# 31 panels of block 2 in high and low parts, the delta rule's inversion rounds in another order, and three norms run together

## The reference, cut to what matters

```
proj = h @ w_in                     # also the 3 x 1024 gate columns br_gate
y_a = mamba2_branch(...)
y_b = stick_breaking_branch(...)    # q, k = rms_norm(q), rms_norm(k), then attention
y_c = gated_deltanet_branch(...)    # o = rms_norm(delta rule) * silu(gate)
branch_proj = einsum("bsie,ied->bsid", stack([y_a, y_b, y_c]), w_branch)
merged = sum(sigmoid(br_gate) * branch_proj, axis=2)
x = x + gate_m * (merged @ w_out)
h = rms_norm(x) * (1 + scale_f) + shift_f
x = x + gate_f * hier_moe(h, ...)
```

## Time and profile before

| what | value |
|---|---|
| median of 3 runs | 1633.55 us (1627.95 to 1636.26) |
| profiled execution | 1627.25 us, its span 1625.4 us |
| TensorE busy | 1531.1 us (94% of the span) |
| VectorE, ScalarE, GpSimd busy | 714.0, 537.9, 217.3 us |
| mean granted TensorE clock | 0.968 of full speed |
| DMA | 375.76 MB, mean 231 GB/s |

### The profile page before, as it was taken

The page is one execution under the profiler, slowest core; times in us unless marked ns, Lnnn a source line. Parts: engine busy times, 40 slices in busy tenths (PEclk is TensorE's granted clock), DMA queues, the critical chain, the costliest instruction groups (busy, mean ns, idle before and its releaser), DMA issues.

```text
span 1625.4 us, 27552 instructions
## 1 busy us (share of the span) xinstructions
PE 1531.1 (94%) x11006; PEld 1262.3 (78%) x11006; DVE 714.0 (44%) x1309; ACT 537.9 (33%) x860; POOL 217.3 (13%) x90
## 2 busy tenths in 40 slices
PE   7988999999999999999989887998899999999997
PEld 5857999999768999989978876887666666566554
DVE  5954888558576888334535412312311111111111
ACT  2345545453445555366551105202111111111110
POOL 0011211212101212238650000000000000000000
PEclk9979999999999999989999968999799999999999
DMA  7674555664434565625441102344999999999995
GB/s 300 234 272 155 166 166 170 198 229 156 153 125 136 172 191 185 191 82 177 137 136 52 52 26 65 105 155 143 423 426 428 428 429 427 427 427 428 426 427 220
DMA packets 63740, 375.76 MB, mean 231 GB/s; under 512 B 7200, under 2 KB 7456, under 8 KB 48032
## 3 DMA queue, kind: packets, MB, share of 16 engines
q1 hardware_dynamic: 63648, 374.43, 61.3%
HBM read 373.35 MB, written 1.05 MB: 230 GB/s over the span
## 4 chain that ended last, share of the span: by engine, by line
PE 71%; issue 13%; DVE 7%; DMA 5%; ACT 3%; SPq 2%; POOL 0%; POOLq 0%; DVEq 0%; ACTq 0%
PE lin L648 7%; PE lin L649 7%; PE lin L650 7%; PE lin L667 6%; PE mixp L1241 6%; PE mixp L1245 6%; PE stat L1265 6%; DVE mixers L1844 3%; PE lin L1219 3%; PE lin L996 2%; DMA moe_arena<-in_experts 2%; DMA modrow<-in_experts 2%; PE stat L1210 2%; PE stat L648 1%; PE mixp L648 1%
## 5 line engine op out<-in xcount | busy, mean ns | idle before, releaser
L648 PE MATMUL lin<-r_hi,w_hi 128*128 128x256 f32 x1344 | 392.1, 292 | 9.4 <-POOL w_lo L1648 5.1
L649 PE MATMUL lin<-r_lo,w_hi 128*128 128x256 f32 x1344 | 382.6, 285 | 0.0
L650 PE MATMUL lin<-r_hi,w_lo 128*128 128x256 f32 x1344 | 382.4, 285 | 0.0
L648 PEld LDWEIGHTS lin<-r_hi,w_hi 128*128 128x128 f32 x1344 | 260.3, 194 | 17.3 <-POOL w_lo L1648 6.7
L649 PEld LDWEIGHTS lin<-r_lo,w_hi 128*128 128x128 f32 x1344 | 260.4, 194 | 0.8
L650 PEld LDWEIGHTS lin<-r_hi,w_lo 128*128 128x128 f32 x1344 | 260.2, 194 | 0.0
L1681 DVE TENSOR_TENSOR w_lo<-ring,w_hi 128x1024 fp32r<-128x1024 f32 x126 | 156.4, 1246 | 84.8 <-ACT w_hi L1312 65.2
L1648 POOL TENSOR_TENSOR w_lo<-ring,w_hi 128x1024 fp32r<-128x1024 f32 x42 | 108.3, 2579 | 480.2 <-ACT w_hi L1312 297.9
L2328 DVE TENSOR_TENSOR moe_arena<-moe_arena,mixp 128x256 f32<-128x256 f32 x32 | 13.5, 421 | 339.2 <-ACT moe_arena L1623 339.2
L1312 ACT ACTIVATE w_hi<-ring 128x1024 fp32r<-128x1024 f32 x124 | 129.6, 1048 | 57.4 <-PE mixp L650 50.0
L667 PE MATMUL lin<-h,ring 128*128 128x256 f32 x640 | 145.5, 385 | 3.0 <-DVE h L1712 3.0
(11 more groups left out here) (422 smaller groups left out, 2641.7 us busy)
## 6 DMA issues: line engine op xcount, KB each, us to landing
ring<-in_panels SPq DMA_DIRECT2D x272, 512.0 KB, 3.5
moe_arena<-in_experts SPq DMA_DIRECT2D x66, 2048.0 KB, 24.5
aring<-in_ada SPq DMA_DIRECT2D x24, 1024.0 KB, 6.1
ring<-in_experts SPq DMA_DIRECT2D x10, 2048.0 KB, 23.2
cst<-in_experts SPq DMA_DIRECT2D x10, 1280.0 KB, 23.0
sq<-in_experts SPq DMA_DIRECT2D x10, 1024.0 KB, 24.6
rs<-in_experts SPq DMA_DIRECT2D x10, 512.0 KB, 25.8
modrow<-in_experts SPq DMA_DIRECT2D x10, 512.0 KB, 28.0
```

Of the source, the lines that this page charges most:

```text
L648: pe.matmul(o, w_hi[:, slot, c], r[0], start=start, stop=False, skip_group_check=True)
L649: pe.matmul(o, w_hi[:, slot, c], r[1], start=False, stop=False, skip_group_check=True)
L650: return pe.matmul(o, w_lo[:, slot, c], r[0], start=False, stop=stop, skip_group_check=True)
```

## The change

`is_split` now also covers the last 31 panels of block 2: branch 2 from j = 1 on (11), branch 1 (12) and the output panels (8). GpSimd makes their low parts. ScalarE cuts a panel when the panel three places ahead of it has been read (`split_hi` in `gates`). Their right-hand sides are split as well: `h` into `r_hi` and `r_lo` behind the state loop, y_c and y_b into `y2_*` and `y1_*`, and `merged` into `c_hi` and `c_lo`, two tiles at a time (`round_merged`). They lie in SBUF where nothing is kept any more by then.

In an inversion round the filling panel moves to behind the first product, the product for `g_d` goes ahead of that for `g_dt`, and the mask of `g_ml` waits only for the first product.

The three norms run together: the Squares of q and k are taken ahead of the rounds, the sums of q, k and the output follow the state loop at once, then three Ln, three Exp and the Silu come in a row. The scaling of the delta rule's output moves behind that of q and k. `gate_branch(2, 0)` and `gate_branch(2, 1)` move behind the two steps of stick-breaking that followed them, and the filling panels are dealt out anew.

```diff
+BRANCHES2 = BRANCH2 + 13
...
-    return OUT0 <= n < BRANCH2
+    return OUT0 <= n < BRANCH2 or BRANCHES2 <= n < PANELS
...
+        with ExitStack() as under_sq:
+            y2_hi, y2_lo = (under_sq.enter_context(nc.sbuf_tensor(n, [P, KH, T], F32R)) for n in ("y2_hi", "y2_lo"))
...
+            with ExitStack() as branch_rows:
+                sb1("below_rows", [P, (8 + KH) * T], stack=branch_rows)
+                c_hi, c_lo = (sb1(n, [P, KD, T], F32R, branch_rows) for n in ("c_hi", "c_lo"))
+                y1_hi, y1_lo = (sb1(n, [P, KH, T], F32R, branch_rows) for n in ("y1_hi", "y1_lo"))
...
+        rs_k, rs_o = gq[:, 0:4, :], gq[:, 4:8, :]
...
-            def split_linear(b, first=False):
+            def split_linear(b, first=False, rows=(r_hi, r_lo)):
...
-                    mm = split_matmul(lin[b][:, 0:T], (b, slice(i * P, (i + 1) * P)), (r_hi[:, i, :], r_lo[:, i, :]),
+                    mm = split_matmul(lin[b][:, 0:T], (b, slice(i * P, (i + 1) * P)), [t[:, i, :] for t in rows],
...
-            def project(rhs):
+            def project(rows, first=False):
...
-                    linear(rhs, 1)
+                    b = split_panel()
+                    bank(b)
+                    split_linear(b, first and m == 0, rows)
+                    panels.advance(1)
...
-            project(None)
+            project((r_hi, r_lo))
...
-            project(None)
+            project((r_hi, r_lo))
...
-                    b = panel()
+                    split = is_split(panels.n)
+                    b = split_panel() if split else panel()
...
+                    if split and (i, j) in ((2, 1), (2, 3), (1, 0)):
+                        pe.wait_ge(h_ready, seen(h_ready, KD if j == 1 else 1))
...
-                        product(b, h)
+                        if split:
+                            split_linear(b)
+                        else:
+                            product(b, h)
+                    elif split:
+                        for m in range(2):
+                            for k in range(KH):
+                                at = (2 * k + m) * P
+                                mm = split_matmul(lin[b][:, m * T:(m + 1) * T], (b, slice(at, at + P)),
+                                                  [t[:, k, :] for t in ((y2_hi, y2_lo) if i == 2 else (y1_hi, y1_lo))],
+                                                  k == 0, k == KH - 1)
+                        mm.then_inc(panel_done, 1)
...
+                branch_panels(0, 3 + n, 4 + n)
...
-                for i, s in blocks:
-                    mm = pe.matmul(stat[:, i, s], g_w[:, i, s], g_dt[:, i, s], start=True, stop=True, skip_group_check=True)
-                mm.then_inc(ev("g_ddt_ready"), 1)
+                if n > 1:
+                    pe.wait_ge(ev("g_dt_ready"), n - 1)
...
-                branch_panels(0, 3 + n, 4 + n)
+                for i, s in blocks:
+                    mm = pe.matmul(stat[:, i, s], g_w[:, i, s], g_dt[:, i, s], start=True, stop=True, skip_group_check=True)
+                mm.then_inc(ev("g_ddt_ready"), 1)
...
+            def head_sums(src, dst):
+                pe.wait_ge(sq_ready, seen(sq_ready))
+                for i in range(4):
+                    mm = pe.matmul(dst[:, i, :], K["ones"], src[:, i, :], start=True, stop=True, skip_group_check=True)
+                mm.then_inc(sums_ready, 1)
+            logs = seen.now(ln_done)
+            head_sums(sq[:, 0:4, :], mixp)
+            pe.wait_ge(ev("g_o_read"), 1)
+            head_sums(sq[:, 4:8, :], stat)
+            pe.wait_ge(ln_done, logs + 1)
+            head_sums(sq[:, 0:4, :], mixp)
+            seen(ln_done, 3)
...
-            pe.wait_ge(ev("g_o_read"), 1)
-            sums(sq, 4, 1)
-            branch_panels(0, 11, 12)
-            sums(sq, 4, 1)
-            pe.wait_ge(ev("yc_done"), 1)
-            branch_panels(2, 0, 2)
-            sums(sq, 4, 1)
+            pe.wait_ge(ln_done, logs + 3)
...
-            branch_panels(2, 2, 3)
+            branch_panels(0, 11, 12)
...
-            branch_panels(2, 3, 6)
+            pe.wait_ge(ev("yc_done"), 1)
+            branch_panels(2, 0, 5)
...
-            branch_panels(2, 6, 8)
+            branch_panels(2, 5, 8)
...
-            project(merged)
+            project((c_hi, c_lo), True)
...
+                    if i != BRANCHES[0]:
+                        split_hi(panels.n + RING - 1)
+            def round_merged(pair, behind):
+                panels.taken(-behind)
+                tiles = slice(2 * pair, 2 * pair + 2)
+                act.activation(c_hi[:, tiles, :], merged[:, tiles, :], ACT.Copy).then_inc(r_hi_ready, 1)
...
+            for half in range(2):
+                tiles = slice(4 * half, 4 * half + 4)
+                act.activation(sq[:, tiles, :], sq_kv[:, tiles, :], ACT.Square).then_inc(sq_ready, 1)
...
-            gates(0, 9, 11)
+            gates(0, 9, 10)
+            act.wait_ge(ev("g_o_ready"), 4)
+            for half in range(2):
+                tiles = slice(4 * half, 4 * half + 4)
+                act.activation(r_hi[:, tiles, :], h[:, tiles, :], ACT.Copy).then_inc(r_hi_ready, 1)
+            def log_sums(dst, src):
+                act.wait_ge(sums_ready, seen(sums_ready))
+                act.activation(dst, src, ACT.Ln, bias=K["eps"], scale=1.0 / P).then_inc(ln_done, 1)
+                seen(ln_done)
+            log_sums(rs[:, :, :], mixp[:, :, :])
...
-            norm(ybr[:, 8:12, :], 4, 4, P)
-            gates(0, 11, 12)
+            act.activation(sq[:, 0:4, :], ybr[:, 8:12, :], ACT.Square).then_inc(sq_ready, 1)
+            log_sums(rs_k, stat[:, :, :])
+            log_sums(rs_o, mixp[:, :, :])
+            act.wait_ge(ln_done, seen.now(ln_done))
+            for t in (rs[:, :, :], rs_k, rs_o):
+                act.activation(t, t, ACT.Exp, scale=-0.5).then_inc(rs_ready, 1)
...
+            next_split[0] = BRANCHES2
+            split_hi(BRANCHES2 + 2)
+            gates(0, 10, 12)
...
-            norm(sq_kv[:, 0:4, :], 4, 4, P)
-            gates(2, 0, 2)
-            act.wait_ge(ev("b_normed"), 1)
-            norm(sq_kv[:, 4:8, :], 4, 4, P)
-            gates(2, 2, 3)
+            act.activation(y2_hi[:, :, :], ybr[:, 8:12, :], ACT.Copy).then_inc(r_hi_ready, 1)
+            split_hi(BRANCHES2 + 3)
...
-            gates(2, 3, 6)
+            split_hi(BRANCHES2 + 4)
+            gates(2, 0, 5)
...
-            gates(2, 6, 12)
-            gates(1, 0, 12)
+            gates(2, 5, 9)
+            act.wait_ge(ev("yb2_done"), 1)
+            act.activation(y1_hi[:, :, :], ybr[:, 4:8, :], ACT.Copy).then_inc(r_hi_ready, 1)
+            gates(2, 9, 12)
+            gates(1, 0, 6)
+            round_merged(0, 6)
+            gates(1, 6, 9)
+            round_merged(1, 6)
+            gates(1, 9, 12)
+            round_merged(2, 6)
+            round_merged(3, 3)
...
-            for n in range(CHAIN2, BRANCH2):
+            for n in (*range(CHAIN2, BRANCH2), *range(BRANCHES2, PANELS)):
...
-                dve.wait_ge(ev("g_ddt_ready"), n)
...
+                    dve.wait_ge(ev("g_w_ready"), n)
...
-                    link(dve.tensor_tensor(g_dt, g_dt, stat[:, :, :], ALU.subtract))
...
+                    dve.wait_ge(ev("g_ddt_ready"), n)
+                    dve.tensor_tensor(g_dt, g_dt, stat[:, :, :], ALU.subtract).then_inc(ev("g_dt_ready"), 1)
...
+                    dve.wait_ge(ev("g_dt_ready"), n)
...
+                    dve.wait_ge(ev("g_ddt_ready"), n)
...
-            dve.wait_ge(ev("g_o_read"), 1)
-            dve.wait_ge(rs_ready, seen(rs_ready))
-            link(dve.scalar_tensor_tensor(ybr[:, 8:12, :], ybr[:, 8:12, :], col("gdn_norm"), rs[:, :, :], ALU.mult, ALU.mult))
-            dve.wait_ge(ev("gg_ready"), 1)
-            dve.tensor_tensor(ybr[:, 8:12, :], ybr[:, 8:12, :], gg, ALU.mult).then_inc(ev("yc_done"), 1)
-            gate_branch(0, 3)
+            for half in range(2):
+                tiles = slice(4 * half, 4 * half + 4)
+                dve.wait_ge(r_hi_ready, seen(r_hi_ready))
+                dve.tensor_tensor(r_lo[:, tiles, :], h[:, tiles, :], r_hi[:, tiles, :].bitcast(F32), ALU.subtract)\
+                    .then_inc(h_ready, 4)
...
-            dve.scalar_tensor_tensor(sq_kv[:, 4:8, :], sq_kv[:, 4:8, :], col("sb_kn"), rs[:, :, :], ALU.mult, ALU.mult)\
+            dve.scalar_tensor_tensor(sq_kv[:, 4:8, :], sq_kv[:, 4:8, :], col("sb_kn"), rs_k, ALU.mult, ALU.mult)\
...
-            gate_branch(2, 0)
+            dve.wait_ge(ev("g_o_read"), 1)
+            dve.wait_ge(rs_ready, seen(rs_ready))
+            link(dve.scalar_tensor_tensor(ybr[:, 8:12, :], ybr[:, 8:12, :], col("gdn_norm"), rs_o, ALU.mult, ALU.mult))
+            dve.wait_ge(ev("gg_ready"), 1)
+            dve.tensor_tensor(ybr[:, 8:12, :], ybr[:, 8:12, :], gg, ALU.mult).then_inc(ev("yc_done"), 1)
+            gate_branch(0, 3)
+            dve.wait_ge(ev("yc_done"), 1)
+            dve.wait_ge(r_hi_ready, seen(r_hi_ready))
```

(17 more changed lines are left out.)

## The result

| | before | after |
|---|---|---|
| median of 4 runs (us) | 1633.61 | 1614.01 |
| ratio, 95% interval | | 0.9882 [0.9864, 0.99] |
| profiled execution (us) | 1627.25 | 1609.74 |
| its span (us) | 1625.4 | 1608.0 |

The forecast was 1616, the gain 17.5 in the profile's times; measured are 19.6 between the medians and 17.51 between the two profiled executions. Lines have new numbers after: L2025 is L2096 (merge), L2023 is L2094, L2151 is L2225, L1652 is L1723 (GpSimd's low parts), L1219 is L1254, and a split panel's matmuls are L656 to L658.

What follows compares the result with a forecast made beforehand. Bound: the chain of waits in block 2 ahead of the first expert load, nearly always on TensorE. Panels 17.8 + rounds 5.2 - norms 5.5 = 17.5 us off the median 1633.55 gives 1616; 8-in-10 range 1602 to 1624.

Steps and rivals of the forecast that it cites:

- Total: Whole kernel: a gain of 17.5 us, from panels, rounds and norms together.
- Rounds: Inversion rounds: the period falls from 10.19 to 8.83 us, the fifth round takes 8.61; net gain 5.24 us.
- Panels and norms together: State loop to `project`: split panels' gain less the stalls and half clock exchanged in norms and stick-breaking, 9.4 us.
- The waits: TensorE idle ahead of (2, 1), (2, 4), (2, 7) and at `settled`: 1.6, 7.1, 5.0 and 2.0 us.
- Half clock behind the long waits: Branch 2: TensorE runs at half clock behind the two long stalls, costing 1.9 us each.
- a scalar_tensor_tensor waits too: VectorE's merges: such an operation waits for a running GpSimd job, up to 2.41 us; called likely, not shown.
- Without GpSimd's jobs: Norms and stick-breaking with split panels and VectorE not held up: stalls of 11.8 instead of 18.5 us, a gain of 6.7.
- Table loads: ScalarE up to `b_l_ready`: each load costs 1.28 us, without the Trainium skill's extra drain of 1.38.
- `project`: Output panels: 8 split panels gain 4.6 us, less a 1.7 us wait for `c_lo` in the first.
- nothing behind it changes: Expert stage: each microsecond taken off ahead of the first expert load moves the end by one.
- the panels brought 17.8 us: Branches 2 and 1 and `project`: 31 panels at 2.88 instead of 3.455 us, a gain of 17.8.
- the norms cost 5.5: Norms and stick-breaking: stalls and half clock of 24.0 us against 18.5, a loss of 5.5.

Runs made afterwards that it cites:

- e0_after: The changed kernel as it is, timed and profiled again: 1612.44 us, ratio to before 0.9877.
- e4: The changed kernel with one more wait on ScalarE, so GpSimd has no job during VectorE's urgent mask and merges: ratio to before 0.984.
- e3: The changed kernel with the 31 panels' low parts made by VectorE instead of GpSimd: ratio to before 0.9848.
- e1: The kernel before with the new order of the inversion rounds alone: 1623.26 us, ratio to before 0.996.
- e2: The changed kernel with its 31 newly split panels put back to float32: ratio to before 0.9856.
- e9: The kernel before with the new norms and stick-breaking alone, old rounds, the 31 panels in float32: ratio to before 0.9923.
- e5: The changed kernel with 12 more instructions in TensorE's program ahead of the expert loop: 1613.36 us, ratio to before 0.9877.
- e7: The changed kernel with e4's wait, both gates ahead of the masks, the third project panel's high part later, and 12 more instructions: 1595.16 us, ratio to before 0.9767.
- e10: e7 again, unchanged: ratio to before 0.9772.
- e8: e7 with panels (2, 1) to (2, 3) left in float32 and without the 12 added instructions: ratio to before 0.977.

## Why the prediction was right, and where not

- **Total.** 17.5 predicted, 17.51 between the profiles. That they agree so closely is luck, twice over. Two errors met in it: the norms gained 2.7 more than forecast in that profile (1.7 in its repeat), the state loop 0.7 more, and 3.9 were lost at the end. And the two profiled executions happened to reach the rounds at the same time (886.66 and 886.61), where others differ by up to 12.6. Between the medians the gain is 19.6, and 20.3 beside e0_after.
- **Rounds.** 5.24 predicted, 5.33 measured (43.85 for 49.18 us of five rounds), and 0.69 more in the state loop, for which the prediction had nothing. The period was 8.81 for 8.83, the fifth round 8.60 for 8.61.
- **Panels and norms together.** Between the state loop and `project` 9.4 were forecast (13.2 from 23 panels, less 3.8), 12.13 measured, 11.1 in e0. The waits: 1.6, 7.1, 5.0 and 2.0 forecast, 0.74, 6.80, 4.29 and 1.50 measured. The places and the order of size were right, each a little too long. GpSimd's jobs are the cause of 3.68 of the 6.80 and of 3.38 of the 4.29 (e4). Half clock behind the long waits cost 1.9 and 1.25, where 1.9 each was forecast. That a scalar_tensor_tensor waits too, left open, is shown: 2.12 at 1003.66.
- **Without GpSimd's jobs** the forecast was a gain of 6.7 in the norms with split panels: e3 gives 123.40 - 13.2 - 104.06 = 6.1.
- **Table loads.** The Ln at 994.65 starts 1.29 behind its load at 993.36, and the softplus ended at 996.23, 27.35 us behind the last matmul of the state loop (968.88), where the sum had 28.05 (974.95 to 1003.0) without drains. The extra drain of 1.38 us per load that the Trainium skill gives ("ScalarE: Activation LUTs", "What ACT_TABLE_LOAD costs") is not seen here either.

```profile
993.36 1.28 ACT L1656 ACT_TABLE_LOAD   x1
994.65 1.58 ACT L1656 ACTIVATE arena<-arena,cst 128x1536 f32<-128x1536 f32 x1
```

- **`project`.** 4.6 less 1.7 forecast, 3.12 measured (the wait for `c_lo` was 1.27 for 1.7).
- **The step that failed: "nothing behind it changes".** The time was taken off ahead of the first expert load as forecast, and more (21.3), but the expert stage grew by 3.9. In the kernels with the 31 panels' instructions as they are (after, e0, e3, e4) it takes 499.8 to 500.5, with 6 added 501.1, and 496.6 to 497.6 in those without them (before, e1, e2, e9), with 12 added (e5, e7, e10) and with 48 less (e8). The 31 panels have 248 more matmuls and as many weight loads (x11254 for x11006), which the page shows as two more packets of instructions; so the last product lies elsewhere in TensorE's program. That this place decides is shown: 6 instructions move the idle by 3 matmuls and 3 weight loads, and 12 take it away. That TensorE waits there for a fetch of instructions was my expectation, and it stays open: the packet moved during the idle is no sign of it, since before and e5_shift12 have one inside the same product too, and run through it.
- **The split of the sum was misleading.** The text reads as if the panels brought 17.8 us and the norms cost 5.5. Taken alone the new norms bring 13.3 (e9), the rounds 6.0 (e1), and the split panels next to nothing, 1.9 us ahead of the expert load, and that is lost again at the end: the changed kernel's stages sum to 721.4 and 722.0, those of e2_float to 719.9. The 17.8 are real as work, but 11.2 came back as idle time ahead of (2, 1), (2, 4) and (2, 7), 3.1 as clock, 1.3 at `c_lo`, 3.4 at the end. I had priced the waits of the new order only beside split panels, never beside the float32 panels that would hide them.

Once the waits are removed the panels pay: e7_best is 16 us under e2_float by stages, and of the waits that the new order can take off e2_float has only 0.63 left.

## What to carry to other kernels

Price a faster piece of work at a place where the engine waits anyway at nothing: ask what ends the wait next, here the chain softplus, mask, merge, before adding up the instructions saved. Work given to GpSimd costs VectorE where an operation with all its operands in SBUF meets it (here merges, masks, a tensor_scalar); a wait that keeps GpSimd's job behind the urgent merges cost nothing and gave 8.7 us. And where two profiles of the same stage differ, look for an idle time of "issue": three microseconds here hung on where a product lies in TensorE's program.

## What was not expected of the hardware

- An idle time of 2.0 to 2.6 us inside a run of TensorE products, waiting for nothing recorded, moved by 3 matmuls when 6 instructions were added ahead of it and gone with 12. In the changed kernel the granted clock behind it was 0.50.
- The stretch ahead of the rounds, in which TensorE does the same in all these kernels, differed by up to 12.6 us between profiled executions. In e0_after the granted clock was 0.93 in the first 200 us and 0.91 from 840 to 880; in e9_norms 0.97 and 1.00.
- The granted clock in the 3 us behind a wait: 0.50 behind 6.80 us of idle and 0.63 behind 4.29 (the changed kernel), 0.55 behind 3.12 and 1.00 behind 0.91 (e4_hold). So a wait shortened from 4.29 to 0.91 gave the clock back as well.
